# A hybrid attention, convolution and expert layer on one core: expert rows stored by an indirect transfer that skips padding rows, pair weights formed behind the ranks, first turned rows evicted ahead of the last tile

## The chip, the core and the metric

The kernel runs on one core of a Trainium2 chip. The metric is the device time in microseconds. The kernel before takes 1632.7 us, the median of three runs (1632.51 to 1635.56). The engines are TensorE (PE in the profile; PEld are its weight loads), VectorE (DVE), ScalarE (ACT), GpSimd (POOL) and SyncE (SP). Each has its own instruction queue, and they wait for each other and for transfers on semaphores. Transfers are issued from SP, ACT and POOL. All of them run on the same 16 DMA engines. In the profile they are the queues q1 (issued by SP), q10 (by ACT) and q0 (by POOL, software-built).

## The reference

One layer on 384 tokens of width 2048: 128 of a prompt and 256 of a sample, all float32.

```
mod = silu(cond) @ w_ada + b_ada                       # 6 rows of 2048 for each of 2 conditions
h = rmsnorm(x)*(1+sc1)+sh1
y = concat(gated_linear_attention(h), hyena_long_convolution(h)) @ w_out
x = x + gt1*rmsnorm(y)
h = rmsnorm(x)*(1+sc2)+sh2
group = argmax(h @ w_router_grp); two best of its 4 experts; weights renormalised times p_group
out = sum over the two experts: gate * ((silu(h@w_gate[e]) * (h@w_up[e])) @ w_down[e])
x = x + gt2*rmsnorm(out)
```

There are 16 experts, each with three 2048 x 512 matrices (12.6 MB), so that the expert stage reads 201 MB of weights. 384 tokens times two experts are 768 expert rows of 2048 numbers (8 KB).

## The kernel before

**The mixer.** SP streams w_in, w_out and w_ada through a small ring of 2 MB slots. w_ada comes in two ways: the first third for TensorE, the rest in "pieces" (1 MB each, two transfers of 512 KB) that VectorE multiplies and adds up itself (`ada_pieces`, L1391 and L1396, 8 instructions a piece). There are two piece buffers, and SP loads a piece when the one before the last is used. A chunk has four pieces. In the first long-convolution block, `ho` = 0, VectorE's order written out by hand is: pieces 2 and 3 of chunk 11, pieces 0 and 1 of chunk 12, `mod_chunks` of chunk 11 (L1360), then `filter_sums`, which waits for the `decay` table (semaphore in_decay) and multiplies the filter taps by it (L1531). TensorE's taps (`filter_taps`, L623) write into banks, one of which is free only after that `mod_chunks` and others only after L1531. TensorE goes on with the projection (L505) behind them in its order.

POOL issues the small transfers. Behind the attention heads its queue holds three fills of 256 rows each: they copy x_sample into the last 768 rows of the DRAM buffer `y_slots` (1792 rows). Then come `decay`, `dft` and the bias row.

**The last projection and the router.** For each of three token tiles, VectorE scales the last quarter of the projection (L1691), ScalarE squares it (L1252), VectorE forms the new residual (L1669), ScalarE squares that (L1114), VectorE scales it (L1674), TensorE turns it (L724) and ScalarE and VectorE evict the turned groups with scale and shift (`h_columns2`, L1231 and L1658). `h_columns2(0)` stands on both engines inside `norm_tile(2)`. Then 32 router matmuls and a chain of small VectorE steps give the two experts, the weights of the pair (`wpair`), the pair masks (semaphore pairs_ready), the ranks (TensorE, L759 and L762), and from these each row's slot, the number of 64-row blocks of each expert, and an index table of 64 rows by blocks. SP meanwhile loads the first weights of the expert stage. It loads two more only after the first indirect gather has landed.

**The expert stage.** The 768 rows are grouped by expert into blocks of 64 slots; a slot without a row is padding. Here there are 18 blocks (1152 slots). Nine slots of 2 MB hold weights, six loads make an expert, and SP issues a load when TensorE has used the slot. For each block POOL gathers the rows (`fetch`, L1047 and L1050; padding rows are out of bounds and skipped), TensorE turns them (L773), multiplies by gate and up (L810), ScalarE and VectorE form the product, TensorE turns it (L820) and multiplies by down (L830). Both engines evict a 64 x 2048 result as `ysl`, 128 partitions by 1024 numbers, and ScalarE stores all 64 rows with two transfers (L1299). The eviction of block b waits until the store of block b-1 has landed.

After the last block POOL gathers the two rows of each token (L1058), the first tile's in two parts (`early_i` for rows stored before the last expert, `late_i` for the others). ScalarE and VectorE combine, normalise and add them, and SP stores the outputs.

## Time and profile before

| | |
|---|---|
| median of three runs | 1632.7 us |
| the profiled execution | 1625.85 us, span 1624.0 us |
| TensorE busy | 1415.5 us (87%) |
| VectorE busy | 744.3 us (46%) |
| ScalarE busy | 239.2 us (15%) |
| POOL busy | 76.8 us (5%) |
| DMA | 421.92 MB, mean 260 GB/s |
| chain that ended last | PE 52%, DMA 22%, DVE 19% |

The span is cut into 40 slices on the page. From slice 27 (about 1055 us) to slice 38 (about 1560 us) the DMA engines are busy nine tenths or more. Before that TensorE is busy nine tenths in most slices. A share of the chain is the time for which the chain of last releasers ran over that engine; a busy share alone says nothing of what bounds a stage.

### The profile page before, as it was taken

Reading aid. Unit: us, or ns where it says so; the run is one execution under the profiler, and the core shown is the slowest. Engines: PE = TensorE matmul, PEld = TensorE weight load, DVE = VectorE, ACT = ScalarE, POOL = GpSimd, SP = SyncE. Lnnn points to the kernel's source line nnn. Section 1 sums busy time; section 2 is a strip of 40 time slices with the busy share of each in tenths; the row PEclk is TensorE's granted clock in tenths of the full one; section 3 lists DMA queues with packets and bytes.
Section 4 is the critical chain, followed back from the end, with each engine's and each line's share of the span. In section 5 each row is a group of like instructions: output and inputs, shape, how many; then the busy total and the mean of one; then the engine's idle time right before and its main releaser. Section 6 shows DMA issues by size and latency. Waiting matters only on the chain.

```text
span 1624.0 us, 13821 instructions
## 1 busy us (share of the span) xinstructions
PE 1415.5 (87%) x5196; PEld 659.3 (41%) x5196; DVE 744.3 (46%) x1239; ACT 239.2 (15%) x390; POOL 76.8 (5%) x127
## 2 busy tenths in 40 slices
PE   2789999999889899999999999579889977999881
PEld 0135544445455555555544444433333332333330
DVE  0144789888857488879793642600000000000005
ACT  1211220100010111211122001511101110111013
POOL 4000000000000100000000000000000000000001
PEclk9699999999889899999999999779999998999885
DMA  9996367677616653322227442999999999999985
GB/s 335 410 354 207 104 226 251 227 260 260 239 50 235 207 165 105 136 65 85 78 73 274 170 155 56 391 351 413 403 362 398 403 397 406 395 413 383 409 342 197
DMA packets 131198, 421.92 MB, mean 260 GB/s; under 512 B 8129, under 2 KB 73892, under 8 KB 113252
## 3 DMA queue, kind: packets, MB, share of 16 engines
q1 hardware_dynamic: 118100, 375.78, 61.0%
q0 software_dynamic: 6656, 32.61, 6.1%
q10 hardware_dynamic: 6384, 12.73, 2.2%
q8 instruction: 40, 0.66, 0.2%
q14 instruction: 18, 0.15, 0.0%
HBM read 409.53 MB, written 23.09 MB: 266 GB/s over the span
## 4 chain that ended last, share of the span: by engine, by line
PE 52%; DMA 22%; DVE 19%; issue 3%; ACT 3%; ACTq 0%; SPq 0%; POOLq 0%; POOL 0%; DVEq 0%
DMA s_mem<-in_w_exp_gate 13%; PE ps L508 12%; PE ps L505 12%; PE ps L810 11%; DVE s_mem L1396 9%; DMA s_mem<-in_w_ada 6%; PE ps L830 6%; DVE s_mem L1546 2%; PE ps L453 1%; PE ps L661 1%; DMA s_mem<-in_hy_freq 1%; PE ps L561 1%; DVE s_mem L1518 1%; PE ps L612 1%; PE ps L580 1%
## 5 line engine op out<-in xcount | busy, mean ns | idle before, releaser
L1396 DVE SCALAR_TENSOR_TENSOR s_mem<-s_mem,s_sT 128x512 f32<-128x512 f32 x480 | 339.4, 749 | 33.0 <-DMA s_mem<-in_w_ada 22.3
L505 PE MATMUL ps<-s_mem 128*128 128x384 f32 x1024 | 335.3, 488 | 1.1 <-DMA s_mem<-in_w_in 1.1
L508 PE MATMUL ps<-s_mem 128*128 128x512 f32 x768 | 334.1, 596 | 0.7 <-ACT s_mem L1216 0.7
L810 PE MATMUL ps<-s_mem 128*64 128x512 f32 x1152 | 265.0, 617 | 32.2 <-DMA s_mem<-in_w_exp_gate 31.5
L505 PEld LDWEIGHTS ps<-s_mem 128*128 128x128 f32 x1024 | 194.6, 191 | 140.8 <-issue 8.4
L508 PEld LDWEIGHTS ps<-s_mem 128*128 128x128 f32 x768 | 145.6, 191 | 183.3 <-issue 182.4
L810 PEld LDWEIGHTS ps<-s_mem 128*64 128x64 f32 x1152 | 90.0, 142 | 204.3 <-issue 203.5
L1799 DVE TENSOR_TENSOR s_mem<-s_mem,ps 64x512 f32<-64x512 f32 x18 | 12.2, 680 | 326.3 <-ACT s_mem L1290 326.3
L830 PE MATMUL ps<-s_mem 128*64 128x512 f32 x576 | 152.5, 690 | 9.3 <-DVE s_mem L1801 9.3
L830 PEld LDWEIGHTS ps<-s_mem 128*64 128x64 f32 x576 | 45.5, 157 | 103.1 <-issue 91.1
L1804 DVE COPY s_mem<-ps 128x512 f32<-128x512 f32 x18 | 12.4, 691 | 156.1 <-PE ps L830 156.1
L1139 ACT ACTIVATE s_mem<-ps 128x512 f32<-128x512 f32 (+1 forms) x61 | 34.2, 580 | 289.9 <-PE ps L508 158.0
L1290 ACT ACT_TABLE_LOAD x18 | 23.1, 1283 | 284.2 <-PE ps L810 284.2
L453 PE MATMUL ps<-s_mem,s_sT 128*32 128x512 f32 x256 | 44.4, 835 | 19.6 <-DMA s_mem<-in_w_ada 19.6
L773 PE MATMUL ps<-s_base,s_mem 64*128 64x64 f32 x304 | 37.5, 276 | 8.1 <-DMA s_mem<-h_rows,s_idx_now 8.1
L773 PEld LDWEIGHTS ps<-s_base,s_mem 64*128 64x128 f32 x304 | 34.9, 200 | 22.8 <-issue 14.6
L612 PE MATMUL ps<-s_mem 128*128 128x512 f32 x96 | 42.9, 596 | 0.7 <-ACT s_mem L1139 0.7
L1191 ACT ACTIVATE s_mem<-ps,s_colB 128x384 f32<-128x384 f32 x24 | 16.1, 671 | 158.0 <-PE ps L505 158.0
L561 PE MATMUL ps<-s_mem 64*128 64x256 f32 x80 | 27.4, 545 | 10.6 <-DVE s_mem L1518 5.7
L1294 ACT ACTIVATE s_mem<-ps 128x512 f32<-128x512 f32 x18 | 10.8, 597 | 171.7 <-PE ps L830 171.7
L1691 DVE TENSOR_TENSOR s_mem<-s_mem,ps 128x512 f32<-128x512 f32 x12 | 8.1, 685 | 60.2 <-PE ps L508 60.0
L1187 ACT ACTIVATE s_mem<-s_mem 128x512 f32<-128x512 f32 x24 | 14.5, 630 | 106.8 <-DVE s_mem L1531 106.8
(258 smaller groups left out, 957.1 us busy)
## 6 DMA issues: line engine op xcount, KB each, us to landing
s_mem<-in_w_ada SPq DMA_DIRECT2D x128, 512.0 KB, 4.8
s_mem<-in_w_exp_up SPq DMA_DIRECT2D x32, 2048.0 KB, 31.6
s_mem<-in_w_exp_gate SPq DMA_DIRECT2D x32, 2048.0 KB, 26.8
s_mem<-in_w_exp_down SPq DMA_DIRECT2D x32, 2048.0 KB, 31.0
s_mem<-in_w_in SPq DMA_DIRECT2D x24, 2048.0 KB, 9.3
s_mem<-in_w_ada SPq DMA_DIRECT2D x16, 2048.0 KB, 11.3
s_mem<-in_w_out SPq DMA_DIRECT2D x8, 2048.0 KB, 8.1
y_slots<-s_mem ACTq DMA_DIRECT2D x36, 256.0 KB, 11.0
```

Of the source, the lines that this page charges most:

```text
L453: m = mm(ps[32 * j:32 * j + 32, bank, :], sT[:, k, :], w[:, n, :], start=(k == 0), stop=(k == KT - 1), skip_group_check=True)
L505: m = mm(ps[:, banks[m_], 0:TOK], v[:, k, m_ * P:(m_ + 1) * P], hT[:, kk, :], start=(kk == 0), stop=(kk == KT - 1))
L508: m = mm(ps[:, banks[m_], :], hT[:, kk, m_ * P:(m_ + 1) * P], v[:, k, :], start=(kk == 0), stop=(kk == KT - 1))
L561: m = mm(ps[:, 4 - d, 0:DV], ksT[d][r:r + CHUNK, c // 2, h * DK:(h + 1) * DK], vtm[r:r + CHUNK, c // 2, h * DV:(h + 1) * DV], start=True, ...
L612: mm(ps[:, bank, :], dft[:, table, :], src, start=True, stop=True).then_inc(filled(key), 1)
L773: m = tr(ps[:, 2 + i, q * BLK:(q + 1) * BLK], hg[:, k:D:KT], ident[0:BLK, 0:BLK])
L810: m = mm(ps[half, 0, :], hgT[:, kh * 8 + k, :], weights(e, 2 * kh + which)[:, k, :], start=(kh + k == 0), stop=(kh * 8 + k == KT - 1), ski ...
L830: m = mm(ps[half, 4 + n // 2, :], heT[:, 2 * kh + k, :], weights(e, 4 + kh)[:, k, n * NCOL:(n + 1) * NCOL], start=(kh + k == 0), stop=(kh ...
L1139: a.op(A(dst, ps[:, b, 0:n], func), freed("act", key))
L1290: A(sg, ps[BLK:2 * BLK, 0, :], ACT.Silu).then_inc(S("sg_ready"), 1)
L1396: v.op(ve.scalar_tensor_tensor(out=o, in0=w, scalar=scale, in1=o, op0=ALU.mult, op1=ALU.add), S("piece_used") if last else None)
L1546: v.op(ve.reciprocal(temps[4 + s], ps[:, b, :]), freed("dve", f"norm{ho}{s}"))
```

## The change

Three edits. First, POOL stores the expert rows with one indirect transfer a block. The store table `store_i` has 128 rows, one for each half row of 1024 numbers; entries of padding slots lie out of bounds. A second group of small matmuls (`index_low`) and three VectorE steps form it. The store of block b-2 stands behind the gather of block b in POOL's loop, and two more stores behind the loop. The four 512-wide columns of the down product are placed so that each partition of `ysl` holds one contiguous half row (4 KB). The buffer is filled whole beforehand: 7 fills of 256 rows in place of 3, at the same place in POOL's queue. Second, the five steps that form `wpair` stand behind pairs_ready. Third, ScalarE's `h_columns2(0)` stands ahead of the square of the last tile's last quarter, behind that square's wait for VectorE (L1691).

```diff
+FILLS = Y_ROWS // DEC
+            take(pe, 6, "index_low")
+            mm(ps[BLK:P, 6, 0:MAXB + 1], ones[:, 0:BLK], none_row, start=True, stop=False)
+            for i in range(2 * NT):
+                m = mm(ps[BLK:P, 6, 0:MAXB + 1], r_tok[:, i, :], r_blk[:, i, :], start=False, stop=(i == 2 * NT - 1))
...
-                        for n in range(4):
-                            half = slice(BLK * (n % 2), BLK * (n % 2 + 1))
-                            m = mm(ps[half, 4 + n // 2, :], heT[:, 2 * kh + k, :],
+                        for n in (0, 2, 1, 3):
+                            half = slice(BLK * (n // 2), BLK * (n // 2 + 1))
+                            m = mm(ps[half, 4 + n % 2, :], heT[:, 2 * kh + k, :],
...
-            for i in range(3):
-                rows = slice((NE * BLK) + i * DEC, (NE * BLK) + (i + 1) * DEC)
-                pool.dma_start(y_dram[rows, :], T["x_sample"][0]).then_inc(S("y_filled"), 16)
+            for i in range(FILLS):
+                rows = slice(i * DEC, (i + 1) * DEC)
+                pool.dma_start(y_dram[rows, :], T["x_sample"][0]).then_inc(S("y_stored"), 16)
...
+            def store(i):
+                pool.wait_ge(S("y_read_act"), i)
+                pool.nop(nofuse=True)
+                pool.wait_ge(S("y_read_dve"), i)
+                pool.nop(nofuse=True)
+                nc.gpsimd.tensor_copy(store_now[:, :], store_i[:, bass.ds(i, 1)]).then_inc(S("store_in"), 1)
+                pool.wait_ge(S("store_in"), i + 1)
+                pool.nop(nofuse=True)
+                pool.indirect_dma_start(out=y_halves, out_offset=bass.IndirectOffsetOnAxis(ap=store_now[:, :], axis=0),
+                                        in_=ysl.rearrange("p a n -> p (a n)"), in_offset=None,
+                                        bounds_check=2 * Y_ROWS - 1, oob_is_err=False).then_inc(S("y_stored"), 16)
-            with pool.Fori(0, nblk) as b:
+            with pool.Fori(0, 2) as b:
+                fetch(b)
+            pool.wait_ge(S("store_rows"), 1)
+            for _ in range(2):
+                pool.sem_inc(S("store_in"), 1)
+            with pool.Fori(2, nblk) as b:
                 fetch(b)
+                store(b)
...
+            store(nblk)
-            pool.wait_ge(S("y_stored"), last * 32 + 1)
+            pool.wait_ge(S("y_stored"), last * 16 + 16 * FILLS)
...
             gather_y(early_i, range(1))
+            store(nblk + 1)
...
-                if t == 2:
-                    h_columns2(0)
...
                     wait_read(act, "dve", key)
...
+                    if (nb, t) == (3, 2):
+                        h_columns2(0)
...
-                act.wait_ge(S("y_stored"), b * 32 + 1)
+                act.wait_ge(S("y_stored"), b * 16 + 16 * FILLS)
                 A(ysl[:, 0, :], ps[:, 4, :], ACT.Copy).then_inc(S("y_read_act"), 1)
-                act.wait_ge(S("y_read_act"), b + 2)
-                act.wait_ge(S("y_read_dve"), b + 2)
-                rows = y_dram[bass.ds(b * BLK, BLK), :].rearrange("r (a c n) -> r a c n", a=2, c=2)
-                for c in range(2):
-                    act.dma_start(rows[:, :, c, :], ysl[c * BLK:(c + 1) * BLK, :, :]).then_inc(S("y_stored"), 16)
...
-            step(ve.tensor_tensor(r_t1, r_m2, r_top, ALU.add))
-            step(ve.reciprocal(r_t1, r_t1))
-            step(ve.tensor_tensor(r_pg, r_pg, r_t1, ALU.mult))
-            step(ve.tensor_tensor(wpair[:, 0, :], r_pg, r_top, ALU.mult))
-            step(ve.tensor_tensor(wpair[:, 1, :], r_pg, r_m2, ALU.mult))
...
             step(ve.tensor_tensor(r_pair, r_one[:, 0], r_one[:, 1], ALU.add), S("pairs_ready"))
+            step(ve.tensor_tensor(r_t1, r_m2, r_top, ALU.add))
...
+            v.op(ve.tensor_scalar(r_store[0:BLK, :], ps[0:BLK, b, 0:MAXB], float(TOK), 2.0 * NO_ROW, ALU.is_ge, ALU.mult),
+                 freed("dve", "index"))
+            b = read(dve, "index_low")
+            step(ve.tensor_scalar(r_store[BLK:P, :], ps[BLK:P, b, 0:MAXB], float(TOK), 2.0 * NO_ROW, ALU.is_ge, ALU.mult),
+                 freed("dve", "index_low"))
+            v.op(ve.tensor_tensor(store_i[:, 2:MAXB + 2], r_store, store_row, ALU.add), S("store_rows"))
```

## Rows read from the trace of the kernel before

**Rows 1.** Windows: busy time (instructions) by engine, granted clock, DMA share, GB/s.

```profile
1066.00:1562.00 496.00, 440.44 (x2004) 170.07 (x2004) 30.53 (x51) 60.93 (x86) 19.83 (x35) 0.93 1.00 399
...
1060.00:1070.00 10.00, 5.57 (x26) 2.92 (x28) 0.00 (x0) 1.19 (x2) 1.16 (x2) 0.50 0.68 246
```

**Rows 2.** The chain that ended last, 530 to 680 us: start, length, what.

```profile
574.71 5.22 DMA s_mem<-in_w_ada
...
586.24 2.44 PE ps L623 x6
588.68 10.52 PE ps L505 x32
```

**Rows 3.** DMA queues and issues, 1065 to 1560 us; landing of L1299's stores.

```profile
q1 hardware_dynamic: 12514, 182.36, 90.9%
q10 hardware_dynamic: 4651, 8.48, 4.6%
q0 software_dynamic: 1392, 6.00, 4.4%
...
s_mem<-h_rows,s_idx_now POOLq DMA_INDIRECT x17, 10.7
...
y_slots<-s_mem ACTq DMA_DIRECT2D x1, 256.0 KB, 9.9
...
DMA to landing us min/median/max: 3.1/11.0/16.4
```

**Rows 4.** Timeline of POOL, 543 to 559 us: start, length, instruction, idle before.

```profile
543.20 1.51 POOL L997 DMA_DIRECT2D y_slots<-in_x_sample  x3
557.91 0.79 POOL L1001 DMA_DIRECT2D s_mem<-in_k_decay  x1 [13.19 <-ACT s_mem L1179]
```

**Rows 5.** Landing: fills (L997), decay, first piece; packets from 545 to 563 us.

```profile
DMA to landing us min/median/max: 9.4/15.5/20.9
...
s_mem<-in_k_decay POOLq DMA_DIRECT2D x1, 768.0 KB, 9.7
...
s_mem<-in_w_ada SPq DMA_DIRECT2D x2, 512.0 KB, 4.1
...
DMA packets 116, 5.33 MB, mean 296 GB/s; under 512 B 33, under 2 KB 33, under 8 KB 34
```

**Rows 6.** Timelines of SP and VectorE, 568 to 590 us.

```profile
568.44 6.79 SPq L876 DMA_DIRECT2D s_mem<-in_w_ada  x4
...
574.50 0.88 DVE L1391 TENSOR_SCALAR s_mem<-s_mem,s_sT 128x512 f32<-128x512 f32 x2 [0.23 <-DVE s_mem L1396]
...
579.96 5.76 DVE L1396 SCALAR_TENSOR_TENSOR s_mem<-s_mem,s_sT 128x512 f32<-128x512 f32 x8 [0.22 <-DMA s_mem<-in_w_ada]
...
586.21 3.68 DVE L1531 TENSOR_TENSOR s_mem<-ps,s_mem 128x512 f32<-128x512 f32 x6
```

**Rows 7.** Timelines of ScalarE and VectorE, 1019 to 1026 us.

```profile
1019.02 0.60 ACT L1252 ACTIVATE s_mem<-ps 128x512 f32<-128x512 f32 x1 [2.21 <-DVE s_mem L1691]
...
1020.20 2.89 ACT L1231 ACTIVATE s_mem<-ps,s_modT 128x128 f32<-128x128 f32 x8
1023.18 1.91 ACT L1114 ACTIVATE s_mem<-s_mem 128x2048 f32<-128x2048 f32 x1
...
1022.79 2.64 DVE L1658 TENSOR_SCALAR s_mem<-ps,s_modT 128x128 f32<-128x128 f32 x8
```

**Rows 8.** Timeline of VectorE in the router, 1044 to 1050 us.

```profile
1044.71 0.16 DVE L1744 TENSOR_TENSOR s_mem<-s_mem 128x3 f32<-128x3 f32 x1
...
1045.71 0.74 DVE L1752 TENSOR_TENSOR s_mem<-s_mem 128x12 f32<-128x12 f32 x8
...
1049.03 0.26 DVE L1758 TENSOR_TENSOR s_mem<-ps,s_base 128x96 f32<-128x96 f32 x1 [2.34 <-PE ps L762]
```

**Rows 9.** Timeline of POOL: an indirect gather in the loop, the first late gather.

```profile
1067.00 0.98 POOL L1050 DMA_INDIRECT s_mem<-h_rows,s_idx_now  x1 [0.82 <-POOL s_idx_now L1047]
...
1591.97 0.99 POOL L1058 DMA_INDIRECT s_mem<-y_slots,s_late_i  x1 [14.82 <-DMA y_slots<-s_mem]
```

More of the change, by code:

```diff
@@ L75, in shape_constants @@
     rows[BLK + MAXB + 2] = -0.5
+    i_half = np.arange(P)[:, None]
     tokens = np.arange(P)[:, None] + P * np.arange(NT)[None, :] - TOK
-    base = np.concatenate([ident, tri, sel.reshape(P, 2 * P), total, np.tile(rows, (P, 1)), tokens], 1).astype(np.float32)
+    store = 2 * (i_half % BLK + BLK * np.arange(MAXB)[None, :]) + i_half // BLK
+    base = np.concatenate([ident, tri, sel.reshape(P, 2 * P), total, np.tile(rows, (P, 1)), tokens, store],
+                          1).astype(np.float32)
     masks = np.zeros((P, 2, P), np.int32)
@@ L257, in build @@
         r_step, r_blk, r_tok = small(2 * NT, MAXB + 2), small(2 * NT, MAXB + 1), small(2 * NT, BLK)
+        r_store = small(MAXB)
         r_sel = at(rt_at[0], NT, EPG * NG)
@@ L1754, in _ @@
             step(ve.tensor_tensor(r_pair, r_one[:, 0], r_one[:, 1], ALU.add), S("pairs_ready"))
+            step(ve.tensor_tensor(r_t1, r_m2, r_top, ALU.add))
+            step(ve.reciprocal(r_t1, r_t1))
+            step(ve.tensor_tensor(r_pg, r_pg, r_t1, ALU.mult))
+            step(ve.tensor_tensor(wpair[:, 0, :], r_pg, r_top, ALU.mult))
+            step(ve.tensor_tensor(wpair[:, 1, :], r_pg, r_m2, ALU.mult))
             b = read(dve, "rank")
```

17 lines of the change are left out of this document (10 added, 7 removed).

## The prediction

> **What bounds the kernel now.** I read the windows first, by stage. In the expert stage the DMA engines' share is 1.00 over 496 us at 399 GB/s [rows 1]: bytes and transfer time set the pace there, not TensorE. The queues split that time: over the 495 us from 1065 to 1560, SP's weights take 90.9%, ScalarE's stores 4.6%, POOL's gathers 4.4% [rows 3]. What a store saves comes off the end, as long as the saving is in DMA time.
>
> Then I read the chain of waits upstream of it. Between 530 and 680 us it runs over VectorE's pieces, one of them waiting for its load, then over the taps on TensorE and straight into the projection [rows 2]. There a late transfer is late at the end: TensorE has nothing else in its order. From the taps to 1000 us the chain goes on over TensorE and VectorE, and TensorE is busy nine tenths in most of the page's slices, so a delay has nowhere to be made up.
>
> Last, the timelines of the places that the edits touch: POOL's fills, the last tile, the router, the end.
>
> **The stores.** Removed: 34 of 36 store transfers in the window, with 4.6% x 495 = 22.8 us of all engines' time. Added: 17 indirect stores. Of the 1152 slots 768 hold rows, so two thirds of the bytes. By ScalarE's price per byte the new ones cost 15.2 us, a saving of 7.6. A 4 KB piece may cost less than two of 2 KB: up to 9. By POOL's price, 21.8 us for 6.00 MB of gathered rows [rows 3], some 5.9 MB of stored rows cost 21.5, a saving of 1. A store from SBUF is nearer to ScalarE's row than a gather is. Against that stands balance: if rows are dealt to 16 engines in order of slot, a block of 36 rows gives some engines three and some two, and the fullest decides. I take 6 us, bounds 1 and 9.
>
> The wait of the next eviction is not at risk: a store is issued at the end of a block and must land by the end of the next, some 25 us later, and the slowest of 36 stores landed after 16.4 us [rows 3]. On POOL the store stands behind a gather whose wait is over earlier in the same block, and the next gather waits for a turn half a block later; two POOL steps and an issue are 0.18 + 0.82 + 0.98 = 2 us [rows 9]. The different order of the down product moves no byte and counts nothing. The 14 small matmuls of `index_low` run while TensorE waits for the first gather, which landed 4.9 us after issue; uncovered they would cost under 2 us. One VectorE step stands ahead of the release of that gather: 0.2 us.
>
> **The fills.** Four more, on POOL's queue ahead of `decay`, `dft` and the bias. The three fills were issued at 543.2, 543.7 and 544.2 [rows 4] and landed 9.4, 15.5 and 20.9 us later [rows 5], so at 552.6, 559.2 and 565.1: 6.25 us each from one to the next. `decay`, issued at 557.9, landed after 9.7 us, at 567.6: 2.5 us behind the last fill. It stood in line. Seven fills end at 565.1 + 4 x 6.25 = 590.1, and `decay` lands at 592.6 or later. VectorE needs it at 586.2 [rows 6]. That alone is 6.4 us, with no cover.
>
> The pieces fare worse. The load of the next piece was issued at 568.4 [rows 6], after the last fill, and landed in 4.1 us [rows 5]. Now 21.7 us of fills are still ahead. How two queues share an engine shows in the expert stage. A lone store lands after 3.1 us; between weight loads the median is 11.0 and one of the first 9.9 [rows 3]. A store is 128 pieces of 2 KB, eight an engine and one for the semaphore. If the queues shared by bytes, 16 KB of store against 16 KB of weights would add 0.6 us. The added 7 us fit nine turns in which each 2 KB waits for one weight packet: 182.36 MB in 12514 packets is 14.6 KB, 0.58 us of an engine. So an engine alternates packet by packet, whatever their size. From 545 to 563 us it ran 83 packets of more than 512 B for 5.33 MB: 64 KB each [rows 5], 3.1 us of an engine at two a fill. A piece is 1 MB in rows of 1 KB, 64 an engine, so in 21.7 us of fills it gets seven of its 64 turns. It lands when the fills are through: 590 plus its own 4 us, near 594.
>
> VectorE began this piece at 574.5 [rows 6], then the next, then the taps' product at 586.2. It begins now at 594: 19.5 us late. `decay` shares the engines with the piece for these last microseconds and is there by 600, well before the taps' product at 606. TensorE stands meanwhile, since its last taps wait for banks that VectorE frees behind both pieces. The term is 19.5 us; bounds 6.4 (`decay` alone) and 24 (`decay`, `dft` and the piece one after the other).
>
> The Trainium skill, DMA: Bandwidth & Descriptors, section Queues, rings and completion order, has each DMA engine go round between queue rows, but drain a whole packet of some 9 to 17 descriptors before it switches. By that rule a piece would need four to seven turns against 64 KB packets instead of 64; the fair-share rival below is that case. The landing of the stores speaks against it: eight descriptors in one turn would not take 9.9 us.
>
> After 20 us of standing TensorE's clock drops. In the window from 1060 to 1070 it first stands and waits for the first gather, works for 5.57 us in all, and the clock is granted at 0.50 (1.2 GHz) to the end [rows 1]. I take four of these microseconds at half speed as the price of such a start: 2 us.
>
> **The last tile.** ScalarE now evicts the turned groups behind its wait for L1691 and ahead of the square: 8 instructions, 2.89 us, between that wait and the start at 1019.02 [rows 7]. Before, they ran while VectorE formed the residual, and ScalarE's next step started at 1023.18, just as both were done. Now the square, its root, the residual and VectorE's eight L1658 (2.64 us, ahead of its next steps in its order) all move by 2.89; ScalarE's next step no longer waits for anything else, and 0.1 us comes back. Term: +2.8. The early release of two banks speeds only TensorE's turning of the second tile, which waits in turn for VectorE's groups. Bounds 0.5 (if the evictions could start before L1691) and 2.9.
>
> **The router.** Five steps from 1044.71 to 1045.71 [rows 8] leave the path to pairs_ready: -1.0. Behind it they lie in VectorE's wait of 2.34 us for the ranks [rows 8]; without that cover the gain would be nil. The first gather is the wait ahead of two loads, and DMA share in 1060 to 1070 is 0.68 [rows 1], so the gain and the 2.8 both reach the DMA stream. Together with the step at the index: +2.0.
>
> **The end.** POOL's late gathers start at 1591.97, released by the landing of ScalarE's last stores [rows 9]. Now POOL copies the index and issues (2 us, of which ScalarE's two issues took about half) before the same landing of about 3 us: +1, bounds 0.3 and 2.
>
> **Sum.** -6 + 19.5 + 2 + 2.0 + 1 = +18.5 us on the profiled execution of 1625.85 (span 1624.0). The median of the runs is 7 us above that execution; put on the median, 1632.7 + 18.5 = 1651.
>
> **Rivals.** Fair share: pieces get half of the engines or several rows a turn. The piece lands by 577 to 586, and `decay` decides, which shares with it and lands at 594 to 597: 8 to 11 us, 1 of clock, with the other terms +6 to +9, so 1640. For it: no row shows 64 KB packets against 1 KB ones. Against: the stores' landing.
>
> Fills hidden: the faster side. If four more fills cost the stretch nothing, because software-built transfers queued behind each other finish at once on free engines, the sum is -6 + 2.0 + 1 = -3, 1630, and with the stores' bound of 9 it is -6. It decides if the seventh fill is through by about 568, in place of 590; the 6.25 us from landing to landing speak plainly against it.
>
> Stores priced as gathers: the fills as forecast, but the indirect store saves 1: 1656. For it: both are indirect transfers by POOL. Against: the direction.
>
> **How the numbers follow.** Forecast 0.55, fair share 0.25, stores as gathers 0.13, hidden fills 0.05, other 0.02. From fair share at its low end with 9 saved (1636) to all high terms (24 + 3 + 2.9 - 1 - 1 + 2, about 1660): I leave out hidden fills and the last of either side and give 1637 to 1659. Within 0.2% (3.3 us, about what a measurement of this kernel tells from no change) 0.04, faster 0.04, slower 0.92.
>
> **What the profile after would show.** Seven fills landing to 590; the piece issued at 568.4 landing after some 25 us; VectorE idle from 574.5 for some 19 us, TensorE standing ahead of L623, L1531 near 606. If L1531 starts at 593 to 597, fair share is right; at 586, hidden fills. In the expert stage POOL's share rises by under 3.1% of the window and ScalarE's 4.6% is gone; L1252 of the last tile starts 2.9 us behind L1691. The prediction is wrong if piece loads overtake the fills.

## The result, and the profile after

The changed kernel takes 1659.0 us (median of 4 runs, 1653.7 to 1661.0) against 1632.6 us for the kernel before beside it (4 runs, 1631.0 to 1635.6): a ratio of 1.0155, interval 1.0127 to 1.0183. It is slower by 26.4 us, where 18.5 were forecast, and lies at the very top of the range, 1637 to 1659. The profiled execution took 1653.66 us (span 1651.8), 27.8 above that of before, so all steps below are read between these two.

A ledger first. The left column is where the program stands; each shift is its start after less its start before.

| place | before | after | shift | step |
|---|---|---|---|---|
| projection on TensorE at the block's start, behind the turned rows (L505 / L514) | 560.05 | 558.47 | -1.6 | -1.6 |
| second six taps on TensorE (L623 / L632) | 586.24 | 609.31 | +23.1 | +24.7 |
| second run of the convolution (L612 / L621) | 611.93 | 637.06 | +25.1 | +2.1 |
| last tile's scaling on VectorE (L1691 / L1719) | 1018.25 | 1044.79 | +26.5 | +1.4 |
| router matmuls (L733 / L742) | 1032.24 | 1061.35 | +29.1 | +2.6 |
| rank matmuls (L759 / L768) | 1046.74 | 1074.85 | +28.1 | -1.0 |
| first gather issued (L1050 / L1064) | 1058.80 | 1087.05 | +28.3 | +0.1 |
| first turned rows (L773 / L782) | 1063.74 | 1093.16 | +29.4 | +1.2 |
| early gather at the end of the stage | 1574.78 | 1604.81 | +30.0 | +0.6 |
| first late gather | 1591.97 | 1619.67 | +27.7 | -2.3 |

Nine tenths of the loss arises in one step. POOL's timeline, after (start, length, instruction, idle before); [rows 4] had three fills:

```profile
541.71 3.45 POOL L1011 DMA_DIRECT2D y_slots<-in_x_sample  x7
556.32 0.79 POOL L1015 DMA_DIRECT2D s_mem<-in_k_decay  x1 [11.16 <-ACT s_mem L1214]
```

Their landing, and the issues of the window from 541 to 562 us (the last number is the median time to landing); [rows 5] before:

```profile
DMA to landing us min/median/max: 9.3/26.5/44.9
...
s_mem<-in_k_decay POOLq DMA_DIRECT2D x1, 768.0 KB, 37.0
```

The seventh fill was issued near 544.7 and the last landing is at about 589.6; `decay` lands at 556.3 + 37.0 = 593.3, in line behind the fills. SP's and VectorE's timelines and a piece of the chain of waits, after:

```profile
566.85 25.63 SPq L890 DMA_DIRECT2D s_mem<-in_w_ada  x4
...
561.06 11.63 DVE L1424 SCALAR_TENSOR_TENSOR s_mem<-s_mem,s_sT 128x512 f32<-128x512 f32 x16
597.70 0.88 DVE L1419 TENSOR_SCALAR s_mem<-s_mem,s_sT 128x512 f32<-128x512 f32 x2 [25.01 <-DMA s_mem<-in_w_ada]
...
609.29 1.89 DVE L1559 TENSOR_TENSOR s_mem<-ps,s_mem 128x512 f32<-128x512 f32 x3
...
567.26 30.34 DMA s_mem<-in_w_ada
```

Read against [rows 6]: the piece issued at 566.85 takes 30.3 us in place of 4.1, VectorE stands for 25.01 us, and L1559 (L1531 before) starts at 609.29 in place of 586.21. TensorE's timeline shows the same stall:

```profile
609.31 3.78 PE L632 MATMUL ps<-s_mem,s_hdn 64*128 64x512 f32 x6 [27.14 <-DVE s_mem L1388]
613.02 11.31 PE L514 MATMUL ps<-s_mem 128*128 128x384 f32 x32
```

The six taps take 3.78 us (2.44 before) and the projection 11.31 (10.52 before, [rows 2]). By windows, the granted clock (third number from the end) was 0.50 in the taps, the lower of the two levels (1.2 GHz), after 27.14 us of standing:

```profile
609.30:613.00 3.70, 3.69 (x6) 1.62 (x6) 3.25 (x5) 2.59 (x5) 0.00 (x0) 0.50 0.84 268
```

The last tile on ScalarE, after ([rows 7] before). The eight evictions now stand between the wait for L1719 and the square of the projection (L1287):

```profile
1045.56 2.90 ACT L1266 ACTIVATE s_mem<-ps,s_modT 128x128 f32<-128x128 f32 x8 [2.20 <-DVE s_mem L1719]
1048.31 0.63 ACT L1287 ACTIVATE s_mem<-ps 128x512 f32<-128x512 f32 x1
```

The router on VectorE ([rows 8] before), and the first gather in the chain of waits. The five steps now lie in a wait that fell from 2.34 to 1.34 us:

```profile
1077.14 0.26 DVE L1788 TENSOR_TENSOR s_mem<-ps,s_base 128x96 f32<-128x96 f32 x1 [1.34 <-PE ps L771]
...
1087.05 6.07 DMA s_mem<-h_rows,s_idx_now
```

The expert stage, by windows (length, busy time and instructions of PE, PEld, DVE, ACT, POOL, granted clock, DMA share, GB/s): the window that answers to [rows 1], the whole stage, and 20 us at each of the two experts that have two blocks.

```profile
1092.00:1588.00 496.00, 439.35 (x2004) 170.37 (x2006) 30.50 (x51) 61.69 (x87) 40.40 (x69) 0.92 0.98 390
...
1093.16:1604.81 511.65, 453.67 (x2068) 176.32 (x2068) 30.88 (x52) 63.95 (x90) 40.40 (x70) 0.92 0.97 389
1233.16:1253.16 20.00, 20.00 (x88) 6.33 (x86) 0.69 (x1) 0.60 (x1) 1.19 (x2) 0.94 0.57 197
1438.16:1458.16 20.00, 20.00 (x90) 6.61 (x88) 0.69 (x1) 0.60 (x1) 1.18 (x2) 0.94 0.82 292
```

The same three windows of the kernel before, counted from its own first turn:

```profile
1063.74:1574.78 511.04, 453.16 (x2068) 176.93 (x2068) 30.88 (x52) 63.94 (x90) 19.83 (x35) 0.92 0.99 395
1203.74:1223.74 20.00, 19.67 (x100) 7.58 (x96) 0.87 (x2) 2.66 (x4) 0.12 (x1) 1.00 0.85 310
1408.74:1428.74 20.00, 19.03 (x96) 7.33 (x93) 1.37 (x2) 3.30 (x5) 0.18 (x1) 0.99 1.00 379
```

And the queues from 1092 to 1587 us after (packets, MB, share of 16 engines), with the stores' row; [rows 3] before:

```profile
q1 hardware_dynamic: 12443, 181.34, 90.4%
q0 software_dynamic: 3700, 11.59, 7.2%
...
y_slots<-s_mem,s_store_now POOLq DMA_INDIRECT x17, 10.6
```

The queues did what was asked of them: 4.6 + 4.4 = 9.0% for stores and gathers became 7.2%. The stage did not get shorter. The DMA share fell instead, from 1.00 to 0.98, and at the two-block experts to 0.57 and 0.82, while TensorE was busy for all 20 us.

The end on POOL ([rows 9] before). Index, issue and landing stand in a row, 5.1 us from copy to late gather:

```profile
1614.57 0.18 POOL L1083 COPY s_store_now<-s_store_i 128x1 int32 x1 [7.41 <-DVE s_mem L1840]
1615.60 1.02 POOL L1086 DMA_INDIRECT y_slots<-s_mem,s_store_now  x1 [0.85 <-POOL s_store_now L1083]
1619.67 1.02 POOL L1072 DMA_INDIRECT s_mem<-y_slots,s_late_i  x1 [3.06 <-DMA y_slots<-s_mem,s_store_now]
```

From the last eviction to the late gather 5.53 us became 6.01: +0.5. The -2.3 of the ledger comes from the last down product, 7.09 us in this execution and 9.82 in that of before; the instructions are the same, the granted clock was 1.00 in this one and 0.72 in that.

### The profile page after: what moved, and what is told of

It reads as the page before. It is cut to its first block, busy times and chain, and to the rows that moved or that the text cites. A ratio compares the mean times of both kernels' runs of the same rounds, so it can differ in the third digit from the quotient of the medians.

```text
span 1651.8 us, 13857 instructions
## 1 busy us (share of the span) xinstructions
PE 1411.8 (85%) x5210; PEld 659.0 (40%) x5210; DVE 744.7 (45%) x1242; ACT 239.0 (14%) x390; POOL 100.5 (6%) x167
## 4 chain that ended last, share of the span: by engine, by line
PE 50%; DMA 23%; DVE 20%; issue 3%; ACT 3%; ACTq 0%; SPq 0%; POOLq 0%; POOL 0%; DVEq 0%
PE ps L514 14%; DMA s_mem<-in_w_exp_gate 12%; PE ps L824 11%; DVE s_mem L1424 10%; DMA s_mem<-in_w_ada 9%; PE ps L517 8%; PE ps L844 6%; DVE s_mem L1574 2%; PE ps L462 2%; PE ps L670 1%; DMA s_mem<-in_hy_freq 1%; DVE s_mem L1546 1%; PE ps L570 1%; PE ps L621 1%; PE ps L632 1%
## 5 line engine op out<-in xcount | busy, mean ns | idle before, releaser
L514 PE MATMUL ps<-s_mem 128*128 128x384 f32 x1024 | 334.4, 487 | 1.1 <-DVE s_mem L1451 1.1
L514 PEld LDWEIGHTS ps<-s_mem 128*128 128x128 f32 x1024 | 194.2, 190 | 141.0 <-issue 8.6
L1835 DVE TENSOR_TENSOR s_mem<-s_mem,ps 64x512 f32<-64x512 f32 x18 | 12.2, 679 | 326.3 <-ACT s_mem L1323 326.3
L1323 ACT ACT_TABLE_LOAD x18 | 23.1, 1283 | 284.3 <-PE ps L824 284.3
L462 PE MATMUL ps<-s_mem,s_sT 128*32 128x512 f32 x256 | 41.5, 786 | 23.2 <-DMA s_mem<-in_w_ada 23.2
L782 PE MATMUL ps<-s_base,s_mem 64*128 64x64 f32 x304 | 37.5, 276 | 8.3 <-DMA s_mem<-h_rows,s_idx_now 8.3
L782 PEld LDWEIGHTS ps<-s_base,s_mem 64*128 64x128 f32 x304 | 34.9, 200 | 23.0 <-issue 14.6
L621 PE MATMUL ps<-s_mem 128*128 128x512 f32 x96 | 42.9, 596 | 0.7 <-ACT s_mem L1174 0.7
L632 PE MATMUL ps<-s_mem,s_hdn 64*128 64x512 f32 x48 | 16.8, 684 | 28.3 <-DVE s_mem L1388 28.3
L1327 ACT ACTIVATE s_mem<-ps 128x512 f32<-128x512 f32 x18 | 10.7, 597 | 169.4 <-PE ps L844 169.4
L1719 DVE TENSOR_TENSOR s_mem<-s_mem,ps 128x512 f32<-128x512 f32 x12 | 8.0, 684 | 59.7 <-PE ps L517 59.5
## 6 DMA issues: line engine op xcount, KB each, us to landing
s_mem<-in_w_exp_up SPq DMA_DIRECT2D x32, 2048.0 KB, 31.3
s_mem<-in_w_exp_down SPq DMA_DIRECT2D x32, 2048.0 KB, 29.9
s_mem<-in_w_in SPq DMA_DIRECT2D x24, 2048.0 KB, 10.1
```

The lines of the kernel that those rows point to most:

```text
L462: m = mm(ps[32 * j:32 * j + 32, bank, :], sT[:, k, :], w[:, n, :], start=(k == 0), stop=(k == KT - 1), skip_group_check=True)
L514: m = mm(ps[:, banks[m_], 0:TOK], v[:, k, m_ * P:(m_ + 1) * P], hT[:, kk, :], start=(kk == 0), stop=(kk == KT - 1))
L621: mm(ps[:, bank, :], dft[:, table, :], src, start=True, stop=True).then_inc(filled(key), 1)
L632: mm(ps[:, uses[key][0], :], hdn[half, t * P:(t + 1) * P], w3[half, :], start=True, stop=True).then_inc(filled(key), 1)
L782: m = tr(ps[:, 2 + i, q * BLK:(q + 1) * BLK], hg[:, k:D:KT], ident[0:BLK, 0:BLK])
```

## The experiments

"Stage" below is the time from the first turned rows to the early gather, in the one profiled execution of each kernel. "Work" is the share of the DMA queues times the stage. Four kernels with the same expert stage (before, `fills7`, `columns`, `fills7_4k`) give stages of 511.0, 512.2, 511.6 and 513.8 us, so differences of stages below some 3 us say nothing. The ratio in the table is not the quotient of the two medians beside it; the two differ by up to 0.2%, which shows how little a difference of 3 us in the times can carry.

| run | median, us | before, us | ratio, interval | stage, us |
|---|---|---|---|---|
| fills7 | 1654.6 | 1631.5 | 1.0148, 1.0108 to 1.0188 | 512.2 |
| fills_early | 1632.7 | 1631.5 | 1.0027, 1.0004 to 1.0049 | 511.3 |
| columns | 1630.2 | 1631.5 | 0.9999, 0.9971 to 1.0027 | 511.6 |
| early_back | 1632.6 | 1631.5 | 1.0003, 0.9981 to 1.0026 | 511.9 |
| store_all | 1637.4 | 1632.9 | 1.0036, 1.0016 to 1.0055 | 516.7 |
| store_none | 1615.8 | 1632.9 | 0.9894, 0.9848 to 0.9939 | 493.9 |
| spread | 1635.1 | 1632.9 | 1.0021, 0.9993 to 1.0049 | 519.6 |
| fills7_4k | 1656.1 | 1632.9 | 1.0157, 1.0105 to 1.0208 | 513.8 |
| act_4k | 1631.1 | 1631.2 | 1.0007, 0.9987 to 1.0027 | 513.5 |
| act_half | 1624.8 | 1631.2 | 0.9969, 0.9948 to 0.9989 | 503.4 |
| act_and_none | 1639.4 | 1631.2 | 1.0048, 1.0025 to 1.0071 | 515.8 |
| early_back_2 | 1634.5 | 1631.2 | 1.0033, 1.0011 to 1.0054 | 509.8 |

**fills7: the kernel before, with seven fills.**

```diff
-            for i in range(3):
-                rows = slice((NE * BLK) + i * DEC, (NE * BLK) + (i + 1) * DEC)
+            for i in range(7):
+                rows = slice(i * DEC, (i + 1) * DEC)
```

> The kernel before with seven fills in place of three, at the same place in POOL's queue; nothing else is changed. Theory (turns by packet: a 1 KB row of a piece waits for a whole 64 KB packet of a fill): the piece issued at about 568 lands 30 us later, the taps (L1531) start 24 to 25 us late, TensorE's slow clock adds 2, and the time is 26 to 27 us above before, all of the change's loss. Rival (fair share by bytes, decay alone late): 8 to 11 us above before, the rest of the change's loss lies elsewhere. Rival (fills hidden): no change.

Measured: 1.0148, +23.1 us. TensorE's and SP's timelines of this kernel:

```profile
612.39 3.78 PE L623 MATMUL ps<-s_mem,s_hdn 64*128 64x512 f32 x6 [23.82 <-DVE s_mem L1360]
...
571.64 24.04 SPq L876 DMA_DIRECT2D s_mem<-in_w_ada  x4
```

The same stall, of 23.82 us, behind the same late piece. The four extra fills alone cost 23 of the 26 us. (The edit's other line makes the first store's wait count seven fills.)

**fills_early: the changed kernel, with four of the fills behind the second attention head.**

```diff
             for h in range(HEADS):
+                if h == 2:
+                    fill(0, 4)
...
-            for i in range(FILLS):
-                rows = slice(i * DEC, (i + 1) * DEC)
-                pool.dma_start(y_dram[rows, :], T["x_sample"][0]).then_inc(S("y_stored"), 16)
+            fill(4, FILLS)
```

> The changed kernel with four of the seven fills issued earlier, behind the second attention head's state store (about 460 us), where no pieces are loaded; the other three stay. Theory (turns by packet): the taps start again at 586, and 26 to 27 us of the loss go: 1631 to 1634. If the fills cost by their bytes wherever they stand, the gain is under 15 us, so 1644 or more. If the loss lies in the indirect stores, there is no gain.

Measured: 1632.7 us, and 1.0027 of the kernel before, interval 1.0004 to 1.0049. Against 1.0155 for the changed kernel that is 1.28%, some 21 us of the loss gone; 26 to 27 were expected. Timelines of POOL, SP and TensorE:

```profile
463.06 2.00 POOL L1001 DMA_DIRECT2D y_slots<-in_x_sample  x4
...
573.61 6.79 SPq L890 DMA_DIRECT2D s_mem<-in_w_ada  x4
...
591.75 3.78 PE L632 MATMUL ps<-s_mem,s_hdn 64*128 64x512 f32 x6 [2.82 <-DVE s_mem L1393]
```

SP's four issues take 6.79 us again, as in [rows 6], where the changed kernel needed 25.63. The same bytes in the same queue cost little 80 us earlier. So it is where the fills stand, not their work, that costs most. That cause is shown from both sides: adding the fills at this place brings the loss, moving them away takes most of it back.

They are not free at the new place either. The first piece issued behind them landed after 12.8 us (median of its two transfers), 4.2 at the same place in the kernel before. Timelines of VectorE and TensorE, `fills_early` and then before:

```profile
495.87 11.63 DVE L1429 SCALAR_TENSOR_TENSOR s_mem<-s_mem,s_sT 128x512 f32<-128x512 f32 x16 [8.28 <-DMA s_mem<-in_w_ada]
...
525.12 0.67 PE L570 MATMUL ps<-s_mem 64*128 64x256 f32 x2 [2.93 <-DVE s_mem L1551]
```

```profile
497.45 0.88 DVE L1391 TENSOR_SCALAR s_mem<-s_mem,s_sT 128x512 f32<-128x512 f32 x2 [0.49 <-DMA s_mem<-in_w_ada]
...
520.70 0.67 PE L561 MATMUL ps<-s_mem 64*128 64x256 f32 x2 [0.85 <-DVE s_mem L1518]
```

VectorE stands for 8.28 us, has slack for most of it, and passes some 2 us on to TensorE. Between the turnings of two neighbouring blocks (L606 and its like, 474.88 and 557.41 in the kernel before) lie 82.3 to 84.0 us in the six traces without early fills, and 85.2 to 85.9 in all eight with them: the early fills cost 2.9 us by the medians, 1.1 at least. Every kernel below but `columns`, `fills7_4k` and `act_4k` has them.

**columns: the kernel before, with ScalarE's first turned groups ahead of the last square.**

```diff
-                if t == 2:
-                    h_columns2(0)
...
+                    if (nb, t) == (3, 2):
+                        h_columns2(0)
```

> The kernel before with only ScalarE's eviction of the first turned rows moved ahead of the last tile's square. Theory: the 2.9 us of the evictions no longer overlap the residual on VectorE; the 32 router matmuls start 2.6 us later (32.2 to 34.8 behind the 1000 us mark) and the time is 2 to 3 us above before (0.15%). Rival (the early release of TensorE's banks makes up for it): router matmuls at the same time, no change.

Measured: 0.9999, interval 0.9971 to 1.0027. ScalarE's timeline:

```profile
1023.69 2.90 ACT L1231 ACTIVATE s_mem<-ps,s_modT 128x128 f32<-128x128 f32 x8 [2.19 <-DVE s_mem L1691]
...
1030.38 1.91 ACT L1114 ACTIVATE s_mem<-s_mem 128x2048 f32<-128x2048 f32 x1 [2.62 <-DVE s_mem L1669]
```

From the middle tile's square, at 1019.17, to the last one's it is 11.21 us. The kernel before has 8.70 there (1014.48 to 1023.18), and `early_back` has 8.69. The edit costs 2.5 us of the path in the trace. The times can't show it: 2.5 us is 0.15%, within the interval.

**early_back: fills_early, with `h_columns2(0)` back at its place. early_back_2: the same kernel again, beside the `act` runs.**

```diff
+                if t == 2:
+                    h_columns2(0)
...
-                    if (nb, t) == (3, 2):
-                        h_columns2(0)
```

> As the run with four early fills, and ScalarE's eviction of the first turned rows back in its old place. Left of the change are the indirect stores, the pair weights behind the ranks, and the early fills. By the sum of the terms, if the stores save 6 us, -6 - 1 + 1: 6 us below before (1626). If the saving of the stores is lost in idle DMA time, as in the changed kernel's expert stage, it is within 2 us of before.

> The kernel of early_back once more, beside act_4k on the same chip, to see by how much the stage and the time of one kernel vary. Stage 511.9 +- 1.5 us; time within 0.3% of before. If the indirect path has a price of its own, act_4k is faster than this by 0 to 3 us although it stores half as many bytes again.

Measured: 1.0003 and 1.0033. This kernel keeps the indirect store with skipping, the moved pair weights and seven fills. Of the two causes of loss found so far the last tile's is gone from it, and of the fills' only the early fills' 2.9 us are left. With 6 us saved it should still have been some 3 us faster. The runs don't show it: the two intervals together allow from 3 us faster to 9 us slower, and less 2.9 us from 6 faster to 6 slower. The next runs asked why.

**store_all and store_none: early_back, with every row stored, and with none.**

```diff
-            v.op(ve.tensor_scalar(r_store[0:BLK, :], ps[0:BLK, b, 0:MAXB], float(TOK), 2.0 * NO_ROW, ALU.is_ge, ALU.mult),
+            v.op(ve.tensor_scalar(r_store[0:BLK, :], ps[0:BLK, b, 0:MAXB], 1.0e6, 2.0 * NO_ROW, ALU.is_ge, ALU.mult),
```

(and the same in the lower half; `store_none` has -1.0 in that place.)

> As the run early_back, but the store table skips nothing: all 64 rows of each block are stored, padding too, 9.44 MB in place of 6.29. Theory A (the fullest engine decides: an engine serves the same few slots in each block and moves its eight half rows whether the others are skipped or not): the stage from the first turn (511.9 us in early_back) to the last weights is as long, within 1 us, and so is the time. Theory B (the mean over the engines decides): 4096-byte writes take 0.16 us each, 17 x 128 of them less 1448 are 728, 7.3 us of all engines: stage and time 5 to 7 us longer than early_back.

> As early_back, but every entry of the store table is out of bounds: no expert row is stored and the output rows are made of filled ones. It bounds what the stores cost. Theory A or B with the DMA engines as the bound: the stage loses 14 to 22 us, 490 to 498 in place of 511.9. Theory C (slots that TensorE holds bound the stage where an expert has two blocks, and what the DMA engines save turns into idle DMA time): the stage stays within 4 us of 511.9 and the DMA engines stand idle for 15 us or more of it (10 in the changed kernel).

Measured: 1.0036 and 0.9894. The stages are 516.7 and 493.9 us, with 511.9 and 509.8 between them for the kernel that skips padding. POOL's queue over each stage, `store_all` first (packets, MB, share):

```profile
q0 software_dynamic: 3840, 14.91, 8.6%
```

```profile
q0 software_dynamic: 3840, 6.01, 4.7%
...
y_slots<-s_mem,s_store_now POOLq DMA_INDIRECT x17, 10.1
```

POOL's work is 8.6% x 516.7 = 44.4 us with all rows, 7.2% x 511.9 = 36.9 with those that count, and 4.7% x 493.9 = 23.2 with none. So skipping takes 7.5 us of work off, and the stage falls by 4.8 to 6.9. In the times it is less clear: 1.0036 became 1.0003 in one run of this kernel and 1.0033 in the other. Leaving the rest out takes 13.7 us of work and 16 to 18 us of the stage, and some 17 us of the time or more. The work of the stores is on the path, and the theory that it isn't has fallen. Two more things stand in these rows. The packet count is 3840 in both, although no row moves in one of them: a skipped entry still leaves its packet. And an indirect store that moves nothing lands after 10.1 us, one with its rows after 10.6 or 10.7, one with all 64 rows after 11.1 (medians).

**spread: early_back, with the rows of a block dealt over the partitions in another order.**

```diff
-    rows = np.concatenate([np.arange(BLK) - BLK,
+    place = np.arange(BLK) % 8 * 8 + np.arange(BLK) // 8
+    rows = np.concatenate([place - BLK,
```

> As early_back, with the rows of a block placed in an order that spreads the filled slots over the 64 partitions (slot p in partition p%8*8 + p//8), so that each group of eight partitions has about as many padding rows as the others. Only constants change. Theory A (fullest engine): a block of 36 rows takes about five turns of the fullest engine in place of eight, the landing of a store falls from 10.6 to 7 or 8 us in the median, and the stage is 3 to 5 us shorter if the DMA engines bound it, unchanged if theory C holds. Theory B: landing and stage unchanged.

Measured: 1.0021, stage 519.6 us, the store's landing 10.7 us (10.6 in `early_back`). If the engine with most rows decided, spreading the padding would have shortened both. It did neither, so the argument of balance in the forecast has no support here. The stage is even 8 to 10 us longer than in the two runs of `early_back`, for the same work, in an execution that took 5.6 us more than this kernel's median. Neither expectation had that, and no run explains it. It warns that a stage of a single execution can be off by more than the 3 us above.

**fills7_4k: fills7, with each fill as two transfers of half rows.**

```diff
-                pool.dma_start(y_dram[rows, :], T["x_sample"][0]).then_inc(S("y_filled"), 16)
+                for c in range(2):
+                    cols = slice(c * D // 2, (c + 1) * D // 2)
+                    pool.dma_start(y_dram[rows, cols], T["x_sample"][0][:, cols]).then_inc(S("y_filled"), 16)
```

> As fills7, but each fill is cut into two transfers of half rows, so that its packets are 4 KB and not 64 KB. Same bytes, same place. Theory (turns by packet): a piece's 1 KB row waits for 4 KB, its 66 turns take about 18 us, it lands near 587 in place of 597, and the taps then wait for decay, near 596: 9 to 13 us above before in place of 23. Rival (shared by bytes, or the piece waits for all earlier transfers in any case): as fills7, 22 to 25 us above before.

Measured: 1.0157, no better than `fills7`. SP's and VectorE's timelines:

```profile
570.55 9.12 SPq L876 DMA_DIRECT2D s_mem<-in_w_ada  x4
...
591.98 0.88 DVE L1393 TENSOR_SCALAR s_mem<-s_mem,s_sT 128x512 f32<-128x512 f32 x2 [15.59 <-DMA s_mem<-in_w_ada]
...
606.32 5.76 DVE L1398 SCALAR_TENSOR_TENSOR s_mem<-s_mem,s_sT 128x512 f32<-128x512 f32 x8 [9.11 <-DMA s_mem<-in_w_ada]
```

The first piece is there about 21 us after its issue in place of 29, since it now takes turns with packets of 4 KB and gets more of them: 1131 in the first 20 us beside 1500 of POOL's queue, where `fills7` has 145 beside 179. But the second piece, which in `fills7` found the fills gone, shares with them too, and VectorE waits another 9.11 us. Together the two cost what the one cost. My expectation, 9 to 13 us above before, had priced the first piece alone, and missed by the second. Turn-taking by the packet is supported by the first piece; the total tells that smaller fill packets are no cure.

**act_4k: the kernel before, with half rows of 4 KB in ScalarE's direct stores, and the pair weights moved.**

```diff
-                        for n in range(4):
-                            half = slice(BLK * (n % 2), BLK * (n % 2 + 1))
-                            m = mm(ps[half, 4 + n // 2, :], heT[:, 2 * kh + k, :],
+                        for n in (0, 2, 1, 3):
+                            half = slice(BLK * (n // 2), BLK * (n // 2 + 1))
+                            m = mm(ps[half, 4 + n % 2, :], heT[:, 2 * kh + k, :],
...
-                rows = y_dram[bass.ds(b * BLK, BLK), :].rearrange("r (a c n) -> r a c n", a=2, c=2)
+                rows = y_dram[bass.ds(b * BLK, BLK), :].rearrange("r (c n) -> r c n", c=2)
                 for c in range(2):
-                    act.dma_start(rows[:, :, c, :], ysl[c * BLK:(c + 1) * BLK, :, :]).then_inc(S("y_stored"), 16)
+                    act.dma_start(rows[:, c, :], ysl[c * BLK:(c + 1) * BLK, :, :].rearrange("p a n -> p (a n)")
+                                  ).then_inc(S("y_stored"), 16)
```

> The kernel before with the pair weights behind the ranks and ScalarE's two stores a block writing contiguous half rows (4 KB packets in place of 2 KB), all 64 rows, three fills, no indirect store. It stores the same bytes in the same packets as store_all, from ScalarE's queue instead of POOL's. If the work of the DMA engines alone decides, the stage from the first turn to the last weights is that of store_all, 516 us, less noise, and the time 0 to 5 us above before. If the indirect path has a price of its own (some 5 us in the stage), the stage is 509 to 512 and the time 1 to 3 us below before.

Measured: 1.0007, stage 513.5 us. (The diff leaves out the five moved steps, which are those of the change.) ScalarE's queue over the stage:

```profile
q10 hardware_dynamic: 2720, 8.92, 4.4%
...
y_slots<-s_mem ACTq DMA_DIRECT2D x34, 256.0 KB, 8.8
```

4.4% x 513.5 = 22.6 us for 8.92 MB. 4 KB packets land sooner (median 8.8 us, 11.0 in [rows 3]) and make the work little smaller. This version is as fast as the kernel before and not faster, although it has no indirect store and no early fills. The stage lies between the two expectations, 509 to 512 for a path with a price and 516 for work alone.

**act_half: act_4k, with only the first halves stored, and seven fills, four of them early.**

```diff
-                for c in range(2):
-                    act.dma_start(rows[:, c, :],
+                for c in range(1):
+                    act.dma_start(rows[:, c, :],
```

> As act_4k, but only the first half row of each expert row is stored, by one transfer a block; the other halves keep what seven fills (four of them early) wrote, so the output rows' second halves are left wrong. DMA work falls by 17 x 64 writes of 0.16 us, 10.9 us of all engines. If work saved by ScalarE's stores comes off the stage at 0.8 to 1 us for each us, as between before (511.0) and store_none (493.9), it takes 501 to 504. If savings of this size turn into idle time at the experts with two blocks whatever the path, 508 to 512.

Measured: 0.9969, and 0.9969 / 1.0007 = 0.9962 of `act_4k`, some 6 us. The stages of `act_4k` and then `act_half`, by windows:

```profile
1068.26:1581.77 513.51, 448.53 (x2068) 175.19 (x2068) 30.51 (x51) 63.56 (x89) 19.82 (x36) 0.93 0.98 393
```

```profile
1070.25:1573.61 503.36, 449.11 (x2066) 175.79 (x2067) 30.53 (x51) 63.11 (x89) 19.83 (x35) 0.93 0.98 392
```

The stage falls by 10.2 us for a store work of 4.4% x 513.5 - 2.2% x 503.4 = 11.5 us less. With direct stores, what is not stored comes off the stage nearly one for one. `act_half` has the early fills and `act_4k` has not; between the two turnings that costs 2.8 us, a part of why the time falls by less than the stage.

**act_and_none: act_4k with seven fills (four early), and beside its direct stores the indirect store of each block with every entry out of bounds.**

```diff
+                act.wait_ge(S("y_act"), b * 32 + 1)
                 A(ysl[:, 0, :], ps[:, 4, :], ACT.Copy).then_inc(S("y_read_act"), 1)
+                act.wait_ge(S("y_read_act"), b + 2)
+                act.wait_ge(S("y_read_dve"), b + 2)
+                rows = y_dram[bass.ds(b * BLK, BLK), :].rearrange("r (c n) -> r c n", c=2)
+                for c in range(2):
+                    act.dma_start(rows[:, c, :], ysl[c * BLK:(c + 1) * BLK, :, :].rearrange("p a n -> p (a n)")
+                                  ).then_inc(S("y_act"), 16)
```

> As act_4k with seven fills (four early), plus POOL's indirect stores with every entry out of bounds: the path without its data, on top of ScalarE's stores. If the indirect path has a price of its own, the stage is 4 to 8 us longer than in act_4k. If not, within 2 us of it.

Measured: 1.0048, interval 1.0025 to 1.0071, against 1.0007, 0.9987 to 1.0027, for `act_4k`: some 6.7 us for eighteen indirect stores that move no row. The intervals just touch. `store_all` against `act_4k` is the same question asked with the rows moving (same bytes, same 4 KB, indirect in place of direct): 1.0036 against 1.0007, some 4.7 us.

Neither pair is clean. Both kernels with the indirect store also have the early fills, and `act_4k` has not. In the traces 2.8 and 3.3 us of the two differences arise between the two turnings named above, 500 us ahead of the first store. What is left for the indirect path is 1 to 4 us in the times, and in the stages 515.8 - 513.5 = 2.3 and 516.7 - 513.5 = 3.2 us. That is no more than the scatter of a stage, and 4 to 8 us had been expected. So a price of the indirect path is not shown. Queue work would be a part of it: POOL's is 4.4% x 515.8 = 22.7 us here, and 4.1% x 513.5 = 21.1 in `act_4k`, 1.6 us more. A clean pair, `act_4k` with the early fills beside `store_all`, was not run.

## Why the prediction was right, and where it was off

The direction, the main cause and the place were right. The size was short by 8 us, mostly by two terms, the fills and the stores. That 1659.0 us still lies at the upper end of the range owes something to luck: the errors of the terms add up to 12 us, and 3 us that no edit accounts for came off in the profiled execution. The upper end itself was added up wrong. The high terms, 24 + 3 + 2.9 - 1 - 1 + 2, are 29.9, which makes 1662.6 us and not "about 1660".

**The fills: forecast 19.5, measured 24.7.** The mechanism was the one given: `decay` in line behind the fills (forecast 592.6 or later, measured 593.3), the seventh landing near 590, the piece held until the fills are through. The mis-sized step is "It lands when the fills are through: 590 plus its own 4 us, near 594". It landed at 597.6. From 589.6 on the piece shares the engines with `decay`, `dft` and the bias, 1.66 MB on POOL's queue, and in place of the 4.1 us of a piece alone ([rows 5]) it needed 8. The queues from 571 to 587 us, while the 64 KB packets ran (packets, MB, share), then from 589.6 to 597.7 us:

```profile
q0 software_dynamic: 112, 5.18, 94.4%
q1 hardware_dynamic: 112, 0.11, 4.2%
...
q1 hardware_dynamic: 1542, 1.53, 59.0%
q0 software_dynamic: 348, 1.36, 44.5%
```

As long as the fills ran, SP's queue got 112 packets to POOL's 112, turn about, and with them 0.11 MB to 5.18. Turn-taking by the packet stands in these two rows, and 112 packets on 16 engines are the seven turns of the forecast. Then it made up 1.53 MB in 8 us, beside 1.36 MB of the tables. The bound of 24 had this case, as `decay`, `dft` and the piece one after the other; the value taken had not. L1559 started at 609.3, forecast near 606. That is 3.6 of the 5.2 us. The other 1.6 are that the block itself began 1.6 us earlier than before, so that 24.7 us of delay left 23.1 at the taps. The forecast's way to the rule was looser than it sounds: nine turns of 0.58 us are 5.2 us, not the 7 that the stores' landing had to explain.

**TensorE's clock: forecast 2, measured 2.1.** The six taps and the projection behind them took 1.3 and 0.8 us more, after 27.14 us of standing. The long stand isn't needed for the first part: in `fills_early` the same six taps took 3.78 us too, at a granted clock of 0.50, behind a wait of 2.82 us.

**The rival of fair share** is out: at its times L1559 would have started at 593 to 597. So is the rival of hidden fills. `fills7` and `fills_early` show the cause with one edit each way.

**The stores: forecast -6, measured +0.6 in the stage.** Two steps failed. The DMA work fell by more than I had allowed: queue shares of (90.1 + 4.7 + 4.3)% x 511.0 = 506.4 us before and (89.9 + 7.2)% x 511.7 = 496.8 after, 9.6 us less, above my bound of 9. But the sentence "What a store saves comes off the end, as long as the saving is in DMA time" is wrong for this change. The engines stood 4.6 us in the stage before and 14.8 after. 9.2 of these 10.2 us lie in the two 20 us windows at the two-block experts: 20 x (0.15 + 0.00) = 3.0 us before, 20 x (0.43 + 0.18) = 12.2 after. There the slots are full, SP can load only when TensorE has used one (at the first of them it waited 39.7 us for TensorE before and 42.2 after), and TensorE has two blocks to do on one set of weights. TensorE's timeline ahead of the first of them, before and after, shows a part of why it came no earlier:

```profile
1186.27 8.67 PE L810 MATMUL ps<-s_mem 128*64 128x512 f32 x32 [3.45 <-DMA s_mem<-in_w_exp_gate]
...
1198.99 8.78 PE L830 MATMUL ps<-s_mem 128*64 128x512 f32 x32 [0.52 <-DVE s_mem L1801]
```

```profile
1216.12 10.03 PE L824 MATMUL ps<-s_mem 128*64 128x512 f32 x32 [3.35 <-DMA s_mem<-in_w_exp_gate]
...
1230.25 9.79 PE L844 MATMUL ps<-s_mem 128*64 128x512 f32 x32 [0.52 <-DVE s_mem L1837]
```

The same 32 matmuls took 8.67 and 8.78 us before, 10.03 and 9.79 after, behind a wait of the same length: 2.4 us. The granted clock tells them apart, by windows over the first 32 of before and then of after (0.81 and 0.70; over the second 32 it is 0.80 and 0.71):

```profile
1186.27:1194.80 8.53, 8.53 (x32) 2.80 (x32) 0.00 (x0) 0.00 (x0) 0.00 (x0) 0.81 1.02 434
```

```profile
1216.00:1226.00 10.00, 9.88 (x32) 3.16 (x32) 0.00 (x0) 0.00 (x0) 0.00 (x0) 0.70 1.01 431
```

They lie just ahead of an expert where TensorE is what the loads wait for. Whether the indirect store brings that clock about is not shown. `early_back` takes 10.09 and 9.82 us there at a stage of 511.9; `early_back_2`, the same kernel, takes 8.45 and 8.78 at 509.8. And `fills7`, whose stores are the old ones, takes 10.08 and 9.82 at 512.2, so the lower clock comes without an indirect store.

The runs settle this much. Store work counts (`act_half`, `store_none`), and skipping padding saves some of it (`store_all` to `early_back`: 7.5 us of work, 4.8 to 6.9 of the stage). The rival "stores priced as gathers", a saving of 1, was nearest in size, and its reason was wrong: the bytes were not dearer (`store_all`'s 44.4 less `store_none`'s 23.2 is 21.2 us for 8.9 MB, `act_4k`'s direct 22.6). **Open:** why the kernel with skipping stores is no faster than the kernel before. A price of the indirect path would do it, but what the pairs leave for one, 1 to 4 us, is not clear of their scatter; and `act_4k`, with direct stores, gained nothing either. If there is such a price, the extra packets that take turns between weight packets, POOL's longer chain of steps in each block, and TensorE's clock behind altered waits are all left as causes, and no run here separates them. The idle time of the engines doesn't decide it: 14.8, 13.3 and 10.7 us in three stages with skipping, 7.9 in `store_none`, but 10.3 in `act_4k` with its direct stores.

**The small terms.** The last tile: forecast +2.8, measured +2.6 here and +2.5 in `columns`. The router: forecast -1.0, measured -1.0, and the cover held, with 1.34 us of the wait left. But the forecast let this gain reach the DMA stream, and it did not: the first gather landed after 6.1 us where it was 4.9. Nor did it in the other kernels that have it. In all but one of the fourteen traces, with the edit or without, the first turned rows come 31.3 to 31.8 us after the router matmuls; the gathers issued earlier landed later. (`fills_early` has 30.1.) The step at the index cost 0.1, forecast 0.2. The end: forecast +1, measured +0.5; the clock of the last block hid it. The 14 matmuls of `index_low` left no mark.

**The sum**, term by term against +18.5: fills +5.2, stores +6.6, clock +0.1, last tile -0.2, index -0.1, landing of the first gather +1.2 (put at nothing in the forecast), end -0.5. That makes +30.8. What no edit accounts for is -1.6 at the block's start, +1.4 between the convolution and the last tile, and -2.8 in the last block: -3.0, and with it the +27.8 of the two executions.

## What to carry to other kernels

A transfer that nobody waits for still has a price: what it holds up. Before adding one, list every load that is issued while it is in flight, and compare packet sizes. Here 1 KB rows beside 64 KB packets took 30 us in place of 4, and moving four of the fills 80 us earlier in the same queue took most of the loss away. The 3 us that they cost there showed only in the traces, and had slipped into every comparison built on that kernel. So give a control run every edit of the run that it is set against, the harmless ones too.

In a stage where the DMA engines are full on the average, look for the stretches in which another engine sets the pace; a saving that arrives just ahead of them can turn into idle time. And price a new transfer path with a run in which it moves nothing, beside the old one, before counting on the bytes that it saves.

## What the runs showed of the hardware

- The DMA engines alternated between queues by the packet whatever the packets' size (112 packets of 1 KB to 112 of the queue with the 64 KB ones, above): a piece of 1 MB in 1 KB rows took 30.3 us beside 64 KB packets and about 21 us beside 4 KB ones (`fills7_4k`), against 4.1 us without fills. The Trainium skill, DMA: Bandwidth & Descriptors, section Queues, rings and completion order, has the engine drain a packet of some 9 to 17 descriptors before it switches. The trace does not agree: when the 64 KB packets ended, the piece had had its seven turns an engine, 112 rows of its 1024, and most of it was still to come.
- An indirect store with every entry out of bounds took 10.1 us to land (10.6 or 10.7 with its rows; 10.7 for the empty ones beside direct stores in `act_and_none`), and left as many packets in its queue as the full one (3840 with the gathers, over 17 blocks). Skipping a row saves its bytes, not its turn.
- A direct store of 256 KB landed after 8.8 us in 4 KB packets and 11.0 in 2 KB ones (medians), for nearly the same engine time (22.6 and 24.0 us over the stage).
- The same 32 matmuls behind a wait of 3.4 us took 7.09, 8.45, 8.67, 10.03 or 10.09 us in different executions, one kernel giving both 8.45 and 10.09. A few per mille of this kernel's time hang on that, in either direction.
